# Constant columns streamed between the outputs of a gated linear attention recurrence

## The reference

```
def gla_recurrence(q, k, v, log_a, s0):
    ...
    def step(S, inp):
        qc, kc, vc, gc = inp
        b = jnp.cumsum(gc, axis=2)
        o_inter = jnp.einsum('nhid,nhde->nhie', qc * jnp.exp(b), S)
        ...
        o = o_inter + jnp.einsum('nhij,nhje->nhie', att, vc)
        ...
        S = jnp.exp(b_last[:, :, 0, :])[..., None] * S + jnp.einsum('nhjd,nhje->nhde', kc * jnp.exp(b_last - b), vc)
        return S, o
```

## Time and profile before

| | us |
|---|---|
| median of three runs | 2114.39 |
| the profiled execution | 2109.99 |
| its span, first to last instruction | 2108.3 |
| PE busy | 1973.1 (94% of the span) |
| DVE busy | 893.3 |
| the recurrence, from its first state update to the head sums | 227.9 (1363.9 to 1591.8) |

### The profile page before, as it was taken

The page is one execution under the profiler, slowest core; times in us unless marked ns, Lnnn a source line. Parts: engine busy times, 40 slices in busy tenths (PEclk is TensorE's granted clock), DMA queues, the critical chain, the costliest instruction groups (busy, mean ns, idle before and its releaser), DMA issues.

```text
span 2108.3 us, 31221 instructions
## 1 busy us (share of the span) xinstructions
PE 1973.1 (94%) x13443; PEld 1766.8 (84%) x13443; DVE 893.3 (42%) x1652; ACT 473.2 (22%) x746; POOL 78.4 (4%) x146
## 2 busy tenths in 40 slices
PE   5989999899999789999999899899987899999998
PEld 3767778768788789999999887688876899999997
DVE  3533332244211256363635422336553663636352
ACT  1512131134322132111111223211111311111111
POOL 1000012300120000000000000000000000000000
PEclk7899999589866789999999999877757999999999
DMA  9566644400131122222222454301112222222211
GB/s 355 192 217 224 217 155 153 145 1 1 52 123 47 41 81 81 81 80 80 90 89 94 131 176 146 119 23 63 63 43 105 81 81 80 80 80 85 94 60 45
DMA packets 160173, 218.72 MB, mean 104 GB/s; under 512 B 7271, under 2 KB 131198, under 8 KB 159630
## 3 DMA queue, kind: packets, MB, share of 16 engines
q1 hardware_dynamic: 148814, 177.52, 25.5%
q0 software_dynamic: 11264, 39.86, 5.5%
HBM read 199.66 MB, written 21.76 MB: 105 GB/s over the span
## 4 chain that ended last, share of the span: by engine, by line
PE 89%; DVE 6%; ACT 2%; DMA 2%; issue 1%; SPq 0%; ACTq 0%; DVEq 0%
PE ps L1320 13%; PE ps L1322 13%; PE ps L1319 13%; PE ps L1030 4%; PE ps L1032 4%; PE ps L1031 4%; PE ps L1218 3%; PE ps L905 2%; PE ps L1434 2%; PE ps L1131 2%; PE ps L1117 2%; PE ps L1285 2%; PE ps L1286 2%; PE ps L1288 2%; PE ps L956 1%; PE ps L1146 1%
## 5 line engine op out<-in xcount | busy, mean ns | idle before, releaser
L1319 PE MATMUL ps<-arena_r,wring_r 128*128 128x288 f32 x2048 | 569.3, 293 | 10.1 <-DVE hbuf_r L2056 10.1
L1322 PE MATMUL ps<-arena_r,wring_r 128*128 128x288 f32 x2048 | 434.9, 293 | 0.0
L1319 PEld LDWEIGHTS ps<-arena_r,wring_r 128*128 128x128 f32 x2048 | 386.3, 189 | 10.3 <-issue 10.3
L1322 PEld LDWEIGHTS ps<-arena_r,wring_r 128*128 128x128 f32 x2048 | 330.0, 189 | 0.0
L1320 PE MATMUL ps<-hbuf_r,wring_r 128*128 128x288 f32 x1024 | 287.6, 297 | 0.0
L1320 PE MATMUL ps<-arena_r,wring_r 128*128 128x288 f32 x1024 | 285.3, 295 | 0.0
L1774 ACT ACTIVATE wring_r<-wring 128x2048 fp32r<-128x2048 f32 x64 | 122.6, 1918 | 617.8 <-DMA wring<-in_mlp_w 617.8
L1320 PEld LDWEIGHTS ps<-hbuf_r,wring_r 128*128 128x128 f32 x1024 | 194.4, 190 | 0.0
L1320 PEld LDWEIGHTS ps<-arena_r,wring_r 128*128 128x128 f32 x1024 | 192.4, 188 | 0.0
L2377 DVE SCALAR_TENSOR_TENSOR xbuf<-ps,mod,xbuf 128x288 f32<-128x288 f32 (+1 forms) x128 | 56.1, 480 | 242.6 <-PE ps L1322 242.6
L1030 PE MATMUL ps<-wring_r,xbuf_r 128*128 128x512 f32 x360 | 149.5, 415 | 0.0
(11 more groups left out here) (373 smaller groups left out, 2941.7 us busy)
## 6 DMA issues: line engine op xcount, KB each, us to landing
wring<-in_mlp_w SPq DMA_DIRECT2D x64, 1024.0 KB, 5.2
arena<-in_ada_w SPq DMA_DIRECT2D x40, 1024.0 KB, 6.1
wring<-in_even_w_in SPq DMA_DIRECT2D x14, 1024.0 KB, 7.8
wring<-in_gla_w_in SPq DMA_DIRECT2D x12, 1024.0 KB, 5.4
wring<-in_ada_w SPq DMA_DIRECT2D x4, 2048.0 KB, 27.7
xbuf<-xspill SPq DMA_DIRECT2D x2, 2304.0 KB, 8.6
arena<-in_cache_cmp_kv POOLq DMA_DIRECT2D x16, 256.0 KB, 10.1
wring<-in_cache_diff_k POOLq DMA_DIRECT2D x16, 256.0 KB, 3.0
```

The costliest lines, as they stand in the source:

```text
L1319: pe.matmul(bank, hi, x_hi[:, k, cols], start=k == 0, stop=False)
L1322: mm = pe.matmul(bank, lo, x_hi[:, k, cols], start=False, stop=k == KC - 1)
```

## The change

PE gets a helper `stream` that multiplies 512 constant bfloat16 columns (a mask that lies in SBUF) by a bfloat16 identity, into bank 1, and whose result nobody reads. It is called twice at the head of each `g_out`, ahead of its waits; once before every second sample in the last head's `g_samples`, for both halves; and once before each of the last head's four sample updates. Nothing is removed or moved.

```
+            def stream(times):
+
+                for _ in range(times):
+                    pe.matmul(ps[:, 1, :], identb, cb[:, 2 * P:2 * P + 512], start=True, stop=True)
+
             def g_out(h, c):
 
+                stream(2)
                 if c:
                     pe.wait_ge(s_ready, NCH * h + c)
                     pe.wait_ge(go_mm, NCH * h + c)
...
                     for n in range(NS):
+                        if h + 1 == HC and n % 2 == 0:
+                            stream(1)
                         mm = pe.matmul(o[:, DS * n:DS * n + DS], s0[:, h % 2, n, e * P:(e + 1) * P],
                                        gqe[:, h % 2, SEQ + DS * n:SEQ + DS * n + DS], start=False, stop=True, skip_group_check=True)
                 mm.then_inc(os_mm, 1)
                 pe.wait_ge(gkdm_ready, h + 1)
                 for p in range(4, 8):
+                    if h + 1 == HC:
+                        stream(1)
                     g_states(h, p)
```

## The result

The changed kernel takes 2134.11 us (median of 4 runs, 2129.55 to 2144.57); the kernel before took 2114.27 us beside it (4 runs, 2111.36 to 2119.98). The ratio is 1.0085, 95% interval 1.0056 to 1.0115: slower by some 18 us, where 2130 us (+15.6) was forecast. The profiled execution took 2130.88 us with a span of 2129.2, so 20.9 us more than the one of before.

What follows compares the result with a forecast made beforehand. PE was taken to bound the kernel (89% of the span). Last head +10.7 and heads 0 to 2 +6, say +16 us on 2109.99, gave 2126; with the median 4.4 above that execution, 2130 us, range 2121 to 2141.

Steps and rivals of the forecast that it cites:

- Output 0: Last head: its pair stands inside PE's 5.1 us wait, 0 us; heads 0 to 2: 1.7 us each, 3.8 taken.
- Outputs 1 to 7, 5.3 forecast: Last head, slow clock: 1.7 us for outputs 1 and 3, 3.6 for outputs 2 and 4 to 7.
- Samples and updates: Last head: eight streams among samples at 0.32 us each, 2.6; four at sample updates at 0.7 each, 2.8.
- I take the middle: Heads 0 to 2 together: +6 us, between clock held everywhere (-1.0) and clock falling as now (about +14).
- Outputs 1 to 7, put at 8.4 us: Heads 0 to 2, mostly full clock: 0.45 us per pair minus three waits of 0.14, 2.8 per head.
- What the clock gives back: Heads 0 to 2: pairs holding the clock up would save 4.4 us per head, 13.2 for three.
- The upper end: Heads 0 to 2, clock falling as now: 12.2, plus 1.2 for slow pairs, plus further slow outputs: about +14.
- The sign named for head 0: In the profile after, head 0's slow stretch behind output 2 should be shorter or gone.
- The first (the clock rises in the last head): Rival: clock rises among the last head's outputs and stays, -13 us in all, 2101 us; chance 0.12.
- The second (streams count for nothing with the clock, being a product with an identity): Rival: streams do not act on the clock, all heads pay, +26 us, 2140 us; chance 0.14.
- The third (no change): Rival: some 10 us gained in heads 0 to 2 meets the last head's +10.7, 2115 us; chance 0.10.
- The fourth (all vanish in waits): Rival: the streams disappear in PE's waits in the recurrence and do nothing; chance 0.03.

Runs made afterwards that it cites:

- the second job: The unaltered change measured once more on another chip, against the kernel before: 2127.41 us, ratio 1.0025 (1.0007 to 1.0044).
- the filled waits: Kernels with twelve streams in the last head's wait before update 2; first one, also three before update 3, added to last-head streams alone: 2109.22 us, ratio 0.9943.

## Why the prediction was right, and where its sizes were off

**The last head: right in place and mechanism, 10.7 forecast, 8.6 measured in three executions** (the change twice, the streams in the last head alone).
- Output 0, 0 us: right, its pair went into DVE's wait, 5.1 to 3.0 us.
- Outputs 1 to 7, 5.3 forecast: 3.7 (1565.5 to the samples at 1591.5 is 26.0; before 1553.1 to 1575.4 is 22.3). The step that fell short was that "the pair covers" only the 0.14 of issue: it takes 0.97 itself, where 0.85 was forecast, but it also takes 0.34 off the first two records, whose weight load it covers, so 0.48 for 0.71.
- Samples and updates, 2.6 + 2.8: together 4.9 (21.3 from the samples to the head sums, before 16.4). The update's 0.7 was 0.75, the sample's 0.32 was 0.22.
- Clock at 0.50 from 1545.7 to the head sums: right.

**Heads 0 to 2: the mis-sized terms.** "I take the middle: +6 us (-1 to +14)" became +11.8, then +4.1, +4.0 and +11.6 in four profiled executions of the same instructions.
- Output 0: 2.0 more in each head, where 1.7 was forecast.
- Outputs 1 to 7, put at 8.4 us in three heads: at full clock a pair costs 0.19 net and not 0.4, because it covers a weight load here too, so 21 pairs are 4.0 (an estimate, as some run at the lower clock).
- What the clock gives back, put at 0 to 13.2: the stretch of outputs 1 to 7 grew by 0.9 us in the two executions at 0.75 and shrank by 3.2 and 3.4 in the two at 0.78 and 0.79, so against 4.0 for the pairs the clock gave back some 3 us, or some 7 (estimates).
- "The prompt's scores and the samples of these heads get no stream, so the clock falls there in any case": wrong for the samples, which ran at 1.00 in all three heads of the kernel before (4.5 us each). Samples and sample updates cost 4.9 us more in the executions at 0.75, where the clock falls in the samples of two heads, and 2.3 and 2.7 in the others, where it falls in those of one; no term of the sum stands for that. The pairs need not be its cause: in the kernel with streams in the last head alone, head 1's samples take 6.4 us too.
- The upper end is added up too low: 12.2, 1.2 and a further slow output in each head (1.0 by the earlier trace rows) make 16.4, not 14.

So the middle of +6 was no better founded than its neighbours, and the time of 2134 us came near 2130 in part by luck: the last head cost 2.1 us less than forecast and the other heads 5.8 more, and the second job's ratio, whose middle is some 5 us above before, lies below the forecast's own range of 2121 to 2141 (7 to 27 above). The sign named for head 0, its slow stretch shorter or gone, did not come in the first profile; it came with the pairs in heads 0 to 2 alone.

**The rivals.** The first (the clock rises in the last head): out as put, since pairs at the lower clock never raised it; but its second half, that it then stays, is what the filled waits showed (up to the samples in one, to the head sums in the others with pairs), and its -13 us is close to the 12 us of the first of them (ratio 0.9943), by coincidence: that kernel has 15 streams more in the last head and none in heads 0 to 2, and its trace shows 3.6 us of it in the last head (5.7 less 2.1). The second (streams count for nothing with the clock, being a product with an identity): out, by the twelve streams that raise it, and by the half-row streams that don't. The Trainium skill's remark on transposes ("TensorE: Matmul & The Clock Gate", section "Part 4: PE-mode transpose") so doesn't carry over to a plain product with an identity; the trace of the filled wait shows 1.00 behind twelve of these. The third (no change): the second job's 1.0025 comes near it, but its interval stays above 1. The fourth (all vanish in waits): out, by 20.9 us.

## What to carry to other kernels

In this kernel, work that only keeps the clock up paid where PE waits anyway, in an unbroken run, and with some of it kept up behind (33.0 to 27.7 us from update 2 to the head sums, for 38.7); sprinkled between slow work it was only a cost (47.3). In the last head pairs held a clock that was up and never raised one. Count what is left of the wait before filling it: twelve streams were 2 us too many. Look at which matmuls raised the clock and not at busy time: 98% busy on half the rows left it at 0.50. Read a clock stretch by stretch, since one mean (0.75 before and after) can hide a gain in the outputs and a loss in the samples. And when a kernel with a loop gets slower by more than its edit can explain, look for issue waits at the loop's return and at the packets of instruction transfers before looking for a reason in the edit.

## What was not expected of the hardware

- A loop's returns can cost 7 us each (21.1 us in three, and 25.9 us in all from the head sums to the end) because of 12 matmuls more ahead of the loop; 34 more cost nothing there.
- One weight load of two small records disappears under a 512-column stream ahead of them: they take 0.32 instead of 0.66 us at the lower clock, and 0.17 instead of 0.36 at the upper, so that a pair costs 0.19 us net at full clock (outputs 1.79 us apart with pairs, 1.60 without).
- The key turns of head 0, ahead of which no kernel here differs on PE, start between 1348.9 and 1362.5 us in the profiled executions. A single profile can so be off by 13 us before the change is reached, which is more than most of these edits are worth; stretches between landmarks compare better than start times.
